# Splitting the remaining input projections of the second block's first mixer

## The chip, the core and the metric

The kernel runs on one NeuronCore of a Trainium2 chip. It is one launch for a whole network of two blocks of two layers each. The metric is the device time of one execution in microseconds (us); lower is better. The names of the engines are those of the profile: PE multiplies matrices, DVE is the vector engine, ACT the scalar engine, POOL does little here, and SP's queue issues the loads of the weights.

## The reference, cut to what matters

The first block (two layers) comes before the stretch that the change touches. The second block begins with `mixer_ab`, which projects the 256 tokens `x` (width 1024) by one wide matrix and feeds two attentions:

```python
def mixer_ab(x, w_in, gate_b, conv_w, head_g, w_out, rel_bias):
    p = jnp.einsum('bsd,de->bse', x, w_in)
    aq = p[..., AB_AQ:AB_AK].reshape(Bn, S, A_HEADS, A_HEAD_DIM)
    ak = p[..., AB_AK:AB_AV].reshape(Bn, S, A_HEADS, A_HEAD_DIM)
    av = p[..., AB_AV:AB_BQ].reshape(Bn, S, A_HEADS, A_HEAD_DIM)
    qk = jax.nn.silu(causal_conv(p[..., AB_BQ:AB_BV], conv_w))
    bq = qk[..., :B_WIDTH].reshape(Bn, S, B_HEADS, B_HEAD_DIM)
    bk = qk[..., B_WIDTH:].reshape(Bn, S, B_HEADS, B_HEAD_DIM)
    bv = p[..., AB_BV:AB_BO].reshape(Bn, S, B_HEADS, B_HEAD_DIM)
    bo = p[..., AB_BO:AB_BI]
    bi = p[..., AB_BI:AB_BF] + gate_b[:B_HEADS]
    bf = p[..., AB_BF:AB_PROJ] + gate_b[B_HEADS:]
    ya = dilated_attention(aq, ak, av, rel_bias).reshape(Bn, S, A_WIDTH)
    yb = jax.nn.sigmoid(bo.astype(jnp.float32)) * head_norm(mlstm(bq, bk, bv, bi, bf), head_g)
    y = jnp.concatenate([ya.astype(x.dtype), yb.astype(x.dtype)], axis=-1)
    return jnp.einsum('bse,ed->bsd', y, w_out)
```

The widths of aq, ak, av, bv and bo are 512 each, that of bq and bk together 1024. The first attention has 8 heads, the second 4. Everything is float32. After the mixer come a layer norm, a mixture of experts, and a second layer with another mixer.

## The kernel before

**The weight stream.** All weights lie in one stream of chunks of 128 x 1024 float32 (512 KB). SP loads them in order into a ring of 4 slots (line 2176). A slot is reloaded when the chunk in it was used. There are two ways to use a chunk.

- *Plain:* PE waits for the load and multiplies float32 by float32, straight from the ring. Each such matmul leaves two records in the profile (`XT,ring` or `ring,XT`). The slot is free (`weights_used`) when PE begins the next chunk.
- *Split:* ACT copies the chunk to `W_HI`, rounded to the type fp32r (line 1152); DVE writes the rest, chunk minus `W_HI`, to `W_LO` (line 1521), and the slot is free at that moment (`split_lo`). There are 4 pairs of `W_HI` and `W_LO`. The activations are split in the same way, here into `X_HI` and `X_LO`, once for all that use them (`split_x`). `mm` then issues three fp32r matmuls for each product: high by high, high by low, low by high.

`project` (line 555) makes one tile of 128 features by 256 tokens from one chunk with 8 products of 128 x 128 by 256. `tokens` (line 566) makes two tiles of 128 tokens by 512 features from 4 chunks, with 16 products of 128 x 128 by 512. `chunk` chooses plain or split by whether the activations come as a pair.

**Who splits when.** Each engine runs its own program, a walk over one list of steps (`schedule`, line 2205); an engine passes over the names for which it has no step. ACT and DVE put their splits between their other work by a `Follower`. PE's program is made first, and it notes a *mark* at each result (the key of its PSUM bank) and at the end of each step of the list: how many split chunks PE had begun there. When ACT or DVE pass the same mark in their own order, they first make all splits that the mark allows, that is up to three beyond the last one begun:

```python
def limit(self, mark):
    begun, n = self.marks[mark]
    count = min(begun - 1 + SPLIT, len(self.chunks))
...
def __call__(self, mark):
    while not self.paused and self.next < min(self.splits.limit(mark), self.ceilings[0]):
        self.one()
...
for name, *args in SCHEDULE:
    if name in steps:
        steps[name](*args)
    follow(("step", name, *args))
```

ACT passes a key's mark just behind the evacuation of that bank (`fn_free`), DVE behind its own reads of a bank (`free`). Both pass the step marks, also of the steps that they don't have. Each engine works strictly in its order: a split waits on ACT for its load and a free pair, on DVE for its `W_HI`, and all behind it waits too.

**The stretch of the change.** The order of the steps is:

- `ab_in`: aq (4 chunks), ak (4), av (4). Before the change the first aq chunk is plain (it comes while x is being split), the other seven of aq and ak are split, and av is plain. PE's line 786, ACT's line 1325.
- The first attention. For each head h: `a_scores(h+1)` (PE scores, DVE adds the bias and takes the maximum, ACT exponentials), `bqk_in(h)` (one chunk, the second attention's queries and keys; PE and ACT's evacuation alone, DVE has no such step), `a_norm(h)` (DVE: reciprocal of the sums and two scalings, line 1817), `a_turn(h)` (PE transposes the probabilities, ACT evacuates), and `a_values` behind every odd head.
- `if_in` (plain matmuls by a small matrix that lies in `PAR`), `b_gates` (DVE and ACT), `bo_in` (4 chunks, evacuated by ACT with a sigmoid), `b_conv` (DVE: 32 operations without a mark among them, then ACT's SiLU, then a scaling by DVE), `gate_rows`, `bv_in` (4 chunks).
- The second attention: `b_scores(0)`, and for each head `b_norm_weights`, `b_scores(h+1)`, `b_turn`, `b_values`; then `b_norm` and `y_out` (8 chunks, the first one plain, the others split).

Of the kernel before, what the change touches and what calls it, by code (L numbers as in the profile page):

```python
# [346 lines left out]
def build_program(nc, stream, params, consts, x_in, out, scratch):  # L347
    n_chunks = stream.shape[0] // 128
    with ExitStack() as ctx:
# [154 lines left out]
        def _(pe):  # L504
# [6 lines left out]
            def mm(dst, w, x, start=True, stop=True, done=None):  # L511


                if isinstance(w, tuple):
                    mm(dst, w[0], x[0], start, False)
                    mm(dst, w[0], x[1], False, False)
                    mm(dst, w[1], x[0], False, stop, done)
                    return
                ins = nc.tensor.matmul(dst, w, x, start=start, stop=stop, skip_group_check=True)  # L519
                if done is not None:  # L520
                    ins.then_inc(done, 1)
                    filled(done)
                elif state["release"]:
                    ins.then_inc(state["release"].pop(0), 1)
# [7 lines left out]
            def columns(w, lo, n):  # L532
                return tuple(p[:, lo : lo + n] for p in w) if isinstance(w, tuple) else w[:, lo : lo + n]

            def chunk(split=False, routed=None):

                n = state["n"]
                splits.place(routed)
                state["n"] += 1
                state["release"] += [state["held"]] if state["held"] is not None else []  # L540
                state["held"] = split_used if split else w_used
                if split:
                    i = len(splits.chunks)
                    splits.chunks.append(n)
                    pe.wait_ge(split_lo, i + 1)
                    return W_HI[:, i % SPLIT, :], W_LO[:, i % SPLIT, :]
                pe.wait_ge(arrived[splits.slot[n]], 16 * splits.turn[n])
                return ring_slot(n)

            def take(*key, bank=None):  # L550
                dst = banks.take(pe, key, bank)
                keys[banks.filled(key).name] = key
                return dst, banks.filled(key)

            def project(key, x, n=T, chunks=1, ready=None):

                dst, done = take(*key)
                for c in range(chunks):
                    w = chunk(isinstance(x(0), tuple))
                    for k in range(KT):  # L560
                        last = c == chunks - 1 and k == KT - 1
                        if ready is not None:
                            ready(8 * c + k)
                        mm(dst[:, :n], columns(w, 128 * k, 128), x(8 * c + k), c + k == 0, last, done if last else None)

            def tokens(key, x, tiles):

                dsts = [take(*key, i) for i in range(len(tiles))]
                for c in range(4):
                    w = chunk(isinstance(x(0, 0, 128), tuple))  # L570
                    splits.marks[(*key, "chunks")] = (len(splits.chunks), state["n"])
                    for i, (lo, n) in enumerate(tiles):
                        for k in range(2):
                            last = c == 3 and k == 1
                            mm(dsts[i][0][:n, :], x(2 * c + k, lo, n), columns(w, 512 * k, 512),
                               c + k == 0, last, dsts[i][1] if last else None)
# [27 lines left out]
            def till(name, before):  # L604

                return lambda k: pe.wait_ge(sem(name), before + k + 1)
# [173 lines left out]
            ht = lambda k: HT[:, k, :]  # L780
            x_parts = lambda k: (X_HI[:, k, :], X_LO[:, k, :])
            x_tok = lambda k, lo, n: (X_HI[:, k, lo : lo + n], X_LO[:, k, lo : lo + n])
            ht_tok = lambda k, lo, n: HT[:, k, lo : lo + n]
            TOK2 = [(0, 128), (128, 128)]

            def ab_in():
                for i, name in enumerate(("aq", "ak")):
                    for j in range(4):
                        project((name, j), x_parts if i + j else ht, 256,
                                ready=(lambda k: banks.await_read(pe, ("ff2", DEPTH - 1, 1, k)), till("x_split", 0))[j] if i == 0 and j < 2 else None)  # L790
                tokens(("av",), ht_tok, TOK2)

            def bqk_in(j):
                project(("bqk", j), ht, 256)

            def bo_in(j):
                project(("bo", j), ht, 256)

            def bv_in():
                tokens(("bv",), ht_tok, TOK2)  # L800

            def if_in():
                at = PARAMS["wif"][0]
# [339 lines left out]
        def _(act):  # L1143
# [10 lines left out]
            follow = Follower(splits, split)  # L1154
# [4 lines left out]
            def fn_free(dst, src, f, key, **kw):  # L1159

                nc.scalar.activation(dst, src, f, **kw).then_inc(banks.freed(key), 1)  # L1161
                banks.await_read(act, key)
                follow(key)

            def wait_bank(*key):
                return banks.await_(act, key)

            def evacuate(key, dst, n=T, f=ACT.Copy, rows=128, **kw):
                fn_free(dst, wait_bank(*key)[:rows, :n], f, key, **kw)
# [155 lines left out]
            def ab_in():  # L1325
                for j in range(4):
                    evacuate(("aq", j), AQ[:, j, :], 256, scale=A_SCALE)
                for j in range(4):
                    evacuate(("ak", j), AK[:, j, :], 256)
                for i in range(2):  # L1330
                    evacuate(("av", i), AV[:, i, :], 512)

# [1 line left out]
                evacuate(("bqk", j), BIN[:, j, 3:259], 256)  # L1334

            def bv_in():
                for i in range(2):
                    evacuate(("bv", i), BV[:, i, :], 512)

# [937 lines left out]
```

## Time and profile before

| | us |
|---|---|
| median of 3 runs (lowest, highest) | 2470.76 (2469.97, 2479.4) |
| the profiled execution, its own time | 2478.8 |
| its span, first to last instruction | 2476.9 |
| PE busy | 2289.2 (92%) |
| DVE busy | 1513.8 (61%) |
| ACT busy | 1067.9 (43%) |
| mean granted TensorE clock | 0.952 |

The span is that of one profiled execution. PE's busy time counts overlapping matmuls as one stretch, and their ends are modelled. The granted clock is a share of full speed. A bracket behind an instruction tells how long its engine was idle before it and which engine's work ended that.

### The profile page before, as it was taken

The numbers are of one execution on the slowest core, as the hardware profiler recorded it, in microseconds if no ns is written. First come the engines' busy times: TensorE is split into PE (matmuls) and PEld (weight loads), VectorE is DVE, ScalarE is ACT, GpSimd is POOL, SyncE is SP. The second block draws the span as 40 slices with busy tenths as digits, with TensorE's granted clock in tenths as the row PEclk, the third lists the DMA queues.
The fourth block names the chain that finished last, engine by engine and source line by source line (L and its number), as shares of the span: only waits on it lengthen the run. The fifth ranks groups of instructions, "written<-read, shape, count | busy, mean of one in ns | idle before, by whom it ended". The sixth has DMA issues, their size and how long they took to land.

```text
span 2476.9 us, 36662 instructions
## 1 busy us (share of the span) xinstructions
PE 2289.2 (92%) x13900; PEld 1911.1 (77%) x13900; DVE 1513.8 (61%) x2349; ACT 1067.9 (43%) x1514; POOL 232.4 (9%) x225
## 2 busy tenths in 40 slices
PE   7999898999999989899999779999989796999997
PEld 6677467999767756799976569987768476998775
DVE  2846365655375546676524565589975266658996
ACT  1142442443113244244333244467764254447775
POOL 1814000100271300011000000000000000000000
PEclk9999899999999989999999779999999898999999
DMA  4332123554333112355432134589964413458994
GB/s 156 128 120 77 51 69 119 179 179 170 111 128 117 63 51 77 136 188 189 162 132 97 43 109 146 197 291 348 345 230 171 136 44 112 151 190 319 346 353 178
DMA packets 109807, 396.86 MB, mean 160 GB/s; under 512 B 12088, under 2 KB 14144, under 8 KB 109376
## 3 DMA queue, kind: packets, MB, share of 16 engines
q1 hardware_dynamic: 108576, 393.45, 44.8%
q8 instruction: 111, 1.82, 0.3%
q10 hardware_dynamic: 1056, 1.06, 0.1%
q14 instruction: 64, 0.52, 0.1%
HBM read 393.40 MB, written 1.06 MB: 159 GB/s over the span
## 4 chain that ended last, share of the span: by engine, by line
PE 66%; DVE 20%; ACT 6%; DMA 5%; issue 2%; SPq 0%; DVEq 0%; ACTq 0%
PE psum L519 65%; DVE W_LO L1521 8%; DMA ring<-in_weights 4%; DVE region L1526 2%; ACT W_HI L1152 2%; PE psum L527 1%; DVE RS L1558 1%; DVE region L1529 1%; ACT region L1157 1%; DVE region L1533 1%; DVE SQ L1526 1%; ACT L1161 1%; ACT SQ L1157 1%; DVE HS L1993 1%; ACT L1157 0%
## 5 line engine op out<-in xcount | busy, mean ns | idle before, releaser
L1521 DVE TENSOR_TENSOR W_LO<-ring,W_HI 128x1024 fp32r<-128x1024 f32 x434 | 531.8, 1225 | 240.4 <-ACT W_HI L1152 232.1
L1152 ACT ACTIVATE W_HI<-ring 128x1024 fp32r<-128x1024 f32 x434 | 460.6, 1061 | 369.7 <-PE psum L519 233.5
L519 PE MATMUL psum<-HN,ring 128*128 128x272 f32 (+1 forms) x1600 | 383.7, 401 | 16.0 <-DVE HN L1533 16.0
L519 PEld LDWEIGHTS psum<-HN,ring 128*128 128x128 f32 x1600 | 310.6, 196 | 84.5 <-issue 24.9
L519 PE MATMUL psum<-X_HI,W_HI 128*128 128x256 f32 x800 | 230.0, 287 | 29.4 <-DVE W_LO L1521 26.6
L519 PE MATMUL psum<-X_LO,W_HI 128*128 128x256 f32 x800 | 227.2, 284 | 0.0
L519 PE MATMUL psum<-X_HI,W_LO 128*128 128x256 f32 x800 | 227.1, 284 | 0.0
L1161 ACT ACTIVATE region<-psum 128x272 f32<-128x272 f32 (+9 forms) x227 | 89.5, 394 | 277.1 <-PE psum L519 257.8
L1521 DVE TENSOR_TENSOR W_LO<-SQ,W_HI 128x1024 fp32r<-128x1024 f32 x128 | 156.8, 1225 | 41.1 <-ACT W_HI L1152 37.5
L519 PEld LDWEIGHTS psum<-X_HI,W_HI 128*128 128x128 f32 x800 | 155.7, 195 | 32.9 <-issue 23.2
L519 PE MATMUL psum<-FN_HI,W_HI 128*128 128x272 f32 (+1 forms) x592 | 170.1, 287 | 0.0
L519 PE MATMUL psum<-FN_HI,W_LO 128*128 128x272 f32 (+1 forms) x592 | 169.4, 286 | 0.0
L519 PE MATMUL psum<-FN_LO,W_HI 128*128 128x272 f32 (+1 forms) x592 | 169.1, 286 | 0.0
L1152 ACT ACTIVATE W_HI<-SQ 128x1024 fp32r<-128x1024 f32 x128 | 136.0, 1062 | 69.3 <-PE psum L519 59.4
L519 PE MATMUL psum<-W_HI,XG_HI 128*128 128x512 f32 x384 | 155.4, 405 | 10.0 <-DVE W_LO L1521 9.8
L519 PEld LDWEIGHTS psum<-X_HI,W_LO 128*128 128x128 f32 x800 | 154.6, 193 | 0.0
L519 PEld LDWEIGHTS psum<-X_LO,W_HI 128*128 128x128 f32 x800 | 154.4, 193 | 0.1
L519 PE MATMUL psum<-region 128*32 128x4 f32 (+12 forms) x1360 | 147.7, 252 | 7.2 <-ACT region L1161 5.6
L519 PE MATMUL psum<-W_HI,XG_LO 128*128 128x512 f32 x384 | 151.7, 395 | 0.0
L519 PE MATMUL psum<-W_LO,XG_HI 128*128 128x512 f32 x384 | 151.2, 394 | 0.0
L519 PE MATMUL psum<-F_HI,W_HI 128*128 128x272 f32 (+1 forms) x512 | 146.4, 286 | 0.1
L519 PE MATMUL psum<-F_HI,W_LO 128*128 128x272 f32 (+1 forms) x512 | 146.1, 285 | 0.0
(281 smaller groups left out, 4272.4 us busy)
## 6 DMA issues: line engine op xcount, KB each, us to landing
ring<-in_weights SPq DMA_DIRECT2D x615, 512.0 KB, 4.2
SQ<-in_weights SPq DMA_DIRECT2D x128, 512.0 KB, 5.2
XT<-in_x SPq DMA_DIRECT2D x1, 1088.0 KB, 5.0
CST<-in_consts SPq DMA_DIRECT2D x1, 1082.5 KB, 7.4
SQ<-bias_by_distance ACTq DMA_DIRECT2D x1, 1024.0 KB, 5.2
out<-XT SPq DMA_DIRECT2D x8, 128.0 KB, 1.9
PAR<-in_params SPq DMA_DIRECT2D x1, 572.0 KB, 8.3
bias_by_distance<-MIX ACTq DMA_DIRECT2D x1, 12.0 KB
```

Of the source, the lines that this page charges most:

```text
L519: ins = nc.tensor.matmul(dst, w, x, start=start, stop=stop, skip_group_check=True)
L527: ins = nc.tensor.transpose(dst, src, ident(k))
L1152: lane(nc.scalar.activation(W_HI[:, s % SPLIT, :], ring_slot(n), ACT.Copy), split_hi)
L1157: lane(nc.scalar.activation(dst, src, f, **kw), sem_)
L1161: nc.scalar.activation(dst, src, f, **kw).then_inc(banks.freed(key), 1)
L1521: lane(nc.vector.tensor_tensor(W_LO[:, s % SPLIT, :], ring_slot(n), W_HI[:, s % SPLIT, :].bitcast(F32), ALU.subtract), split_lo)
L1526: lane(nc.vector.tensor_tensor(dst, a, b, op), done)
L1529: ins = nc.vector.tensor_scalar(dst, a, s1, s2, op0) if op1 is None else nc.vector.tensor_scalar(dst, a, s1, s2, op0, op1)
L1533: lane(nc.vector.scalar_tensor_tensor(dst, a, s, b, op0, op1), done)
L1558: lane(nc.vector.reciprocal(ap, ap))
L1993: free(nc.vector.scalar_tensor_tensor(HS[:, :], src[:, :], SLOTG[:, g : g + 1], SGB[:, :], ALU.mult, ALU.mult), "moe", l, "up", e)
```

## The change

Four calls on PE get the split activations in place of the plain ones, so that 20 chunks become split ones: av (4), bqk (8), bo (4), bv (4). ACT passes the mark of the last chunk of av and of bv before it evacuates these two groups. Nothing else changes; order of steps, buffers and stream stay.

```diff
-                tokens(("av",), ht_tok, TOK2)
+                tokens(("av",), x_tok, TOK2)
 
             def bqk_in(j):
-                project(("bqk", j), ht, 256)
+                project(("bqk", j), x_parts, 256)
 
             def bo_in(j):
-                project(("bo", j), ht, 256)
+                project(("bo", j), x_parts, 256)
 
             def bv_in():
-                tokens(("bv",), ht_tok, TOK2)
+                tokens(("bv",), x_tok, TOK2)
@@ ACT, ab_in
                 for j in range(4):
                     evacuate(("ak", j), AK[:, j, :], 256)
+                follow(("av", "chunks"))
                 for i in range(2):
                     evacuate(("av", i), AV[:, i, :], 512)
@@ ACT
             def bv_in():
+                follow(("bv", "chunks"))
                 for i in range(2):
                     evacuate(("bv", i), BV[:, i, :], 512)
```

## Rows read from the trace of the kernel before

**Rows 1.** busy time by stage: us, PE, PEld, DVE, ACT, POOL busy, clock, DMA

```profile
1259.50:1273.40 13.90, 13.90 (x35) 5.97 (x33) 0.00 (x0) 0.98 (x2) 0.00 (x0) 1.00 0.31 111
1275.00:1318.00 43.00, 42.35 (x205) 32.76 (x204) 12.87 (x60) 18.20 (x52) 0.00 (x0) 1.00 0.29 99
1325.20:1353.50 28.30, 28.30 (x101) 18.40 (x100) 19.22 (x42) 9.75 (x13) 0.00 (x0) 1.00 0.43 147
...
1361.00:1388.50 27.50, 21.71 (x48) 12.22 (x48) 11.73 (x49) 6.22 (x14) 0.00 (x0) 0.50 0.00 0
```

**Rows 2.** order of time in the heads: start us, us, engine, what, idle before

```profile
1278.64 0.55 PE L527 MATMUL psum<-CST,GATE 128*128 128x128 f32 x3 [0.65 <-DVE GATE L1529]
1278.80 0.97 ACT L1161 ACTIVATE region<-psum 128x256 f32<-128x256 f32 x2
...
1279.12 0.92 PE L519 MATMUL psum<-region 64*128 64x128 f32 x4
...
1283.95 2.51 PE L519 MATMUL psum<-region 128*64 128x256 f32 x12
...
1287.28 0.17 DVE L1820 RECIPROCAL SM<-SM 128x2 f32<-128x2 f32 x1
...
1287.48 0.68 DVE L1529 TENSOR_SCALAR GATE<-GATE,SM 128x128 f32<-128x128 f32 x2
...
1289.95 0.49 PE L527 MATMUL psum<-CST,GATE 128*128 128x128 f32 x3
1290.21 0.91 ACT L1161 ACTIVATE region<-psum 128x256 f32<-128x256 f32 x2 [1.74 <-PE psum L519]
```

**Rows 3.** order of time from b_conv on, DVE and then PE

```profile
1331.89 0.36 DVE L1529 TENSOR_SCALAR region<-region,PAR 128x256 f32<-128x256 f32 x1
...
1345.94 1.53 DVE L1533 SCALAR_TENSOR_TENSOR region<-region,PAR 128x256 f32<-128x256 f32 x3
...
1351.58 0.17 DVE L1785 COPY region<-psum 128x16 f32<-128x16 f32 x1
...
1361.08 0.90 PE L527 MATMUL psum<-CST,GATE 128*128 128x128 f32 x3 [2.38 <-DVE GATE L1529]
...
1364.69 1.22 PE L519 MATMUL psum<-SQ,CST 4*128 4x256 f32 x2
...
1368.72 0.85 PE L527 MATMUL psum<-CST,GATE 128*128 128x128 f32 x3
```

**Rows 4.** order of time on ACT in the same stretch

```profile
1339.42 0.38 ACT L1161 ACTIVATE region<-psum 128x256 f32<-128x256 f32 x1 [3.07 <-PE psum L519]
...
1353.13 0.21 ACT L1157 ACTIVATE region<-region 128x8 f32<-128x8 f32 x1
```

**Rows 5.** order of time beside split chunks of ab_in, ACT and then DVE

```profile
1242.88 0.38 ACT L1161 ACTIVATE region<-psum 128x256 f32<-128x256 f32 x1 [6.87 <-PE psum L519]
1243.30 1.06 ACT L1152 ACTIVATE W_HI<-ring 128x1024 fp32r<-128x1024 f32 x1
1245.71 0.38 ACT L1161 ACTIVATE region<-psum 128x256 f32<-128x256 f32 x1 [1.35 <-PE psum L519]
...
1244.46 1.23 DVE L1521 TENSOR_TENSOR W_LO<-ring,W_HI 128x1024 fp32r<-128x1024 f32 x1 [2.35 <-ACT W_HI L1152]
```

**Rows 6.** order of time on PE, first and last of c_v's 48 matmuls

```profile
1908.29 0.40 PE L519 MATMUL psum<-W_HI,X_HI 128*128 128x512 f32 x1
...
1919.26 0.39 PE L519 MATMUL psum<-W_HI,X_LO 128*128 128x512 f32 x1
```

**Rows 7.** busy time and clock around two gaps of PE

```profile
170.00:178.00 8.00, 5.08 (x15) 3.92 (x15) 5.51 (x3) 7.71 (x13) 7.12 (x5) 0.79 0.17 62
1475.00:1479.00 4.00, 0.85 (x8) 0.66 (x7) 3.35 (x11) 2.32 (x3) 0.00 (x0) 1.00 0.00 0
1487.00:1491.00 4.00, 4.00 (x22) 4.00 (x21) 1.78 (x2) 1.64 (x3) 0.00 (x0) 0.57 0.39 131
```

**Rows 8.** the page's DMA issues: size and us to landing

```profile
ring<-in_weights SPq DMA_DIRECT2D x615, 512.0 KB, 4.2
```

## The prediction, made before the changed kernel ran

> **What bounds the kernel now.** I read the stages' busy times first [rows 1]. From the value projection on (1259.5 us) the busy share of PE is everything: the eight heads of the first attention (1275 to 1318) have PE at 42.35 of 43.00 us, and gate plus values of the second attention (1325.2 to 1353.5) at 28.30 of 28.30. All of it runs at the full granted clock. DVE and ACT are at 30 to 42% in the heads. Then I read the order of time inside a head [rows 2]: PE goes from turning the probabilities to scores to the next bqk chunk without a break, and DVE's normalising (1287.48, over at 1288.2) is ready 1.8 us before PE wants it at 1289.95. Last I read DVE and ACT of the second attention's start [rows 3, 4]: there PE's bo and bv chunks run beside a DVE chain of almost the same length (b_gates, 15.6 us of b_conv, SiLU, scaling).
>
> **What the change saves on PE.** A plain project chunk costs PE 3.46 us: ACT's evacuation of the last bo (1339.42) is 0.38 long and comes after 3.07 idle, one chunk of PE [rows 4]. A split one costs 2.83 us: the evacuations at 1242.88 and 1245.71 [rows 5]. So 0.63 us less for each of 12 chunks. The plain av group fills 13.9 us [rows 1]; the split c_v group of the same shape goes from 1908.29 to about 1919.5 [rows 6], 48 matmuls at 0.234 = 11.2 us. So 2.7 us less for av and for bv. Were this all, the PE saving would be 12 x 0.63 + 2 x 2.7 = 12.9 us.
>
> **What it adds.** 20 chunks need a W_HI on ACT (1.06 us) and a W_LO on DVE (1.23 us) [rows 5], 21 and 25 us in sum. The idle shares would hold them; their place in the queues does not. Both followers take the split that is three chunks ahead as soon as their own program passes a mark that PE recorded. ACT passes the first mark that allows it, that of ("bqk", h), after evacuating bqk h. DVE has no step bqk_in; it passes the step mark of bqk_in(h), which allows the same split, straight after a_scores(h+1) and before a_norm(h). No earlier mark allows it (the a_scores(h+1) keys were recorded before bqk h was begun). So W_LO waits there for a W_HI that waits for the end of bqk h, behind it stands a_norm(h), and on PE a_turn(h) waits for a_norm(h), with scores of h+2 and bqk h+1 queued behind it. This wait is new, and it is inside the loop.
>
> Its price per head, from the moment PE could go on: 0.26 us to the start of the evacuation (PE goes on at 1289.95, ACT starts at 1290.21 [rows 2]), 0.42 to W_HI's start, 1.16 to W_LO's start, 1.23 of W_LO with 0.03 after it [rows 5], 0.20 from the reciprocal to the scaling and 0.68 of scaling [rows 2], 0.05 to PE: 4.05 us in which PE has nothing. Less the 0.63 saved, each of heads 1 to 7 gets 3.42 us longer: 23.9 us. For head 0 ACT is busy until 1278.80 (a table load and four exponentials); its evacuation of 0.42 starts there, then 0.42 + 1.16 + 1.26 + 0.88 + 0.05 = 3.77, puts the turn at 1282.57 against 1278.64 [rows 2]: 3.9 us. **Heads: +27.8 us.** Bounds of this term: 0 less 5 us saved, if DVE had W_LO behind it in time, and nothing above, since each link has its row. In av the extra follow(("av", "chunks")) lets ACT split before it evacuates, as c_in does: no wait, **-2.7 us**.
>
> **The clock.** The kernel before has such gaps elsewhere: in the 8 us from 170 on PE is busy for 5.08, after a gap of 2.9, and the granted clock is 0.79. Between the two levels (1.2 and 2.4 GHz, 0.50 and 1.00) that makes 0.21 x 2 x 8 = 3.4 us at half. From 1475 PE has 0.85 us of work in 4; the same 3.4 us at half (0.43 x 2 x 4) come there too, but only from 1487 on, beside a full PE [rows 7]. Work that falls into 3.4 us at half speed loses up to 1.7 us. The eight gaps of 4.05 us are of this size. A part of the low stretch lies in the gap itself, and it may also last longer than 3.4 us with only 4 to 6 us of work between gaps. I take 1.7 us for each: **+13.6 us**; bounds 0 and, at 0.50 all through, once more the PE work of the heads (turn 0.42, scores 0.85, bqk 2.83 = 4.1 us, and in every odd head the values, 2.51 - 0.92 = 1.59 more [rows 2]), 39 us.
> The Trainium skill, page "TensorE: Matmul & The Clock Gate", section "HAM oscillation — how this bites in real kernels", says that where every round waits longer than it works, TensorE starts every round at the lower clock. Here the wait (4.05) is about as long as the work (4.1 to 5.7). By the page every round starts slow, and the term is at least the one taken, at most rival (b); the trace's single gaps agree, and no row shows a repeated one.
>
> **Gate and values of the second attention.** All from the end of if_in, 1325.3. Before: DVE starts b_conv at 1331.89, needs 15.6 us (8 groups, 1331.89 to 1347.5), SiLU with table load, scaling and copy to 1351.75, that is 26.45 [rows 3]. After: DVE must do four W_LO, the ones three ahead of bo 0 to 3, between b_gates and b_conv, and the last of them follows the end of bo 3. PE: bo 0 to 3 at 2.83 = 11.3; then 0.26 + 0.42 + 1.16 + 1.26 = 3.1: b_conv starts at 14.4, 7.85 late. The fourth bv chunk has its W_LO only at DVE's step bv_in, behind b_conv; and its W_HI on ACT behind SiLU and the table load for the floors (free 1.6 us after the copy [rows 4]). PE stands still after the third bv chunk, from about 20 to 38. Counting from the copy (34.3): W_HI 1.65 to 2.7, W_LO to 4.0, bv's last chunk 4.0 to 9 or 9.6 (2.8 us at full, 5.6 at half clock). Meanwhile both engines run three more splits: of the last, the ring slot is free at 4.0, its load lands 4.2 later [rows 8], W_HI to 9.4, W_LO to 10.65, and only then may DVE mask the scores of head 0. b_scores(0) and (1) take PE 8.1 us at half clock (4.03 for one, 1364.69 to 1368.72 [rows 3]), about half at full. b_turn(0) thus comes at 14 (full) to 17.6 (half) after the copy, against 9.3 before (1361.08). I take 15.9. **7.85 + 6.6 = +14.4 us**; bounds +12.5 and +16.2, or -2 if the splits were free.
> From b_turn(0) on nothing changes: that part sits at 0.50 already [rows 1], its splits are done, and y_out's first chunk stays plain, so the ring is held where it was.
>
> **Sum.** 27.8 - 2.7 + 13.6 + 14.4 = +53 us. Against the profiled execution (span 2476.9, 2478.8 in all) that is 2532; it ran 8 us above the median of its three runs, and the median is what I add to: 2470.76 + 53 = 2524.
>
> **Rivals.**
> (a) The clock stays full in the heads and in bv's last chunk: 27.8 - 2.7 + 12.5 = +37.6, 2508. For it: after the gap at 1475 the clock stayed full for eight microseconds more [rows 7]. Against: the fall came all the same.
> (b) The clock stays at half all through the heads: 27.8 - 2.7 + 39 + 16.2 = +80, 2551. For it: 1361 to 1388.5 is at 0.50 all the way with PE 79% busy [rows 1]. Against: a round of the heads has bqk's dense matmuls in it, and with such work behind the gap the half clock lasted 3.4 us in both places [rows 7]. The Trainium skill's rule above (page "TensorE: Matmul & The Clock Gate") leads here if a round that starts slow also stays slow.
> (c) The other side: the new W_LO does not stand in the way, since DVE and ACT have 58 to 70% of their time free. Its mechanism is that each split is done one head earlier than I read it, in the time that DVE idles (it has 12.87 us of work in 43 [rows 1]). Then the heads give 8 x 0.63 = 5 us, av 2.7, and bo and bv no more than 2, since the chain over DVE ends at 1351.54 and PE's values at 1353.5, 1.96 us later: 2461. It decides if a_norm(h) comes before the end of bqk h; the order of marks speaks against it.
> (d) Only one of the two places stalls: b_conv alone 14.4 - 2.7 - 5 = +7, 2477; the heads alone 27.8 + 13.6 - 2.7 - 2 = +37, 2507.
>
> **Chances.** Forecast 0.62 (its own range 2512 to 2540), (a) 0.14, (b) 0.10, (c) 0.06, (d) 0.08. Range for 8 in 10: 2503 to 2547. Half a per cent is 12 us, about what a measurement tells from no change: slower 0.91, same 0.04, faster 0.05.
>
> **What would show it.** In the heads: gaps of about 4 us before PE's turn, released by DVE's scaling; DVE idle before W_LO, released by ACT; PE share near 50 to 60%; clock 0.6 to 0.9 there. After if_in: four W_LO between the gate rows and b_conv, DVE's first convolution some 14.4 us after if_in, a PE gap of about 18 us inside bv that ends with W_LO. Wrong if the normalising starts before bqk ends, or if b_conv starts 6.6 us after if_in.

## The result, and the profile after

The changed kernel takes 2535.09 us (median of 6 runs, 2526.53 to 2541.37), the one before 2473.6 (6 runs, 2469.97 to 2483.88): 1.0239 times as long, interval 1.0216 to 1.0262, or 61.5 us more. The profiled execution took 2532.66 with a span of 2530.8, against 2478.8 and 2476.9 before; its mean granted clock is 0.934 against 0.952. The page after, span, busy times and the two kinds of split instruction:

```profile
span 2530.8 us, 36998 instructions
...
PE 2298.4 (91%) x14028; PEld 1932.5 (76%) x14028; DVE 1537.9 (61%) x2369; ACT 1089.2 (43%) x1534; POOL 232.0 (9%) x225
...
L1523 DVE TENSOR_TENSOR W_LO<-ring,W_HI 128x1024 fp32r<-128x1024 f32 x454 | 556.2, 1225 | 285.6 <-ACT W_HI L1152 277.2
L1152 ACT ACTIVATE W_HI<-ring 128x1024 fp32r<-128x1024 f32 x454 | 481.9, 1061 | 372.4 <-PE psum L519 232.9
```

Each split costs what the prediction's rows say (1.23 and 1.06 us), and neither DVE nor ACT is short of time. The stages show where the time went. Windows of the kernel after, columns as in [rows 1]: av; the heads from the first turn to the last; the last turn with if_in; from there to b_turn(0); the first heads of the second attention:

```profile
1258.80:1270.00 11.20, 11.20 (x52) 8.95 (x52) 6.44 (x6) 6.28 (x7) 0.00 (x0) 1.00 0.70 231
1279.00:1361.90 82.90, 55.89 (x237) 46.31 (x237) 19.68 (x58) 21.24 (x48) 0.00 (x0) 0.64 0.13 45
1361.90:1373.50 11.60, 11.56 (x44) 4.98 (x44) 0.47 (x1) 0.87 (x2) 0.00 (x0) 0.74 0.13 47
1373.50:1422.30 48.80, 30.75 (x165) 24.78 (x166) 32.65 (x68) 20.78 (x26) 0.00 (x0) 0.79 0.16 54
...
1422.30:1448.80 26.50, 21.06 (x49) 12.14 (x47) 10.71 (x44) 5.64 (x13) 0.00 (x0) 0.50 0.00 0
```

The av group takes 11.2 us where it took 13.9 [rows 1]. From the first turn (of the probabilities of head 0) to the last the heads take 82.9 us where they took 37.6 (1278.64 in [rows 2] to the first row below); PE is busy for 55.9 of the 82.9, at a clock of 0.64 where it was 1.00 [rows 1]. The last turn and if_in take 2.5 us more (the turn to if_in's end was 9.0), b_turn(0) comes 48.8 us after if_in where it came 35.8 after (1325.3 to 1361.08 [rows 3]). The last row answers to the last of [rows 1], and is much as it was (PE busy for 79% in both, clock 0.50). The turn of head 7, before and after:

```profile
1316.23 0.49 PE L527 MATMUL psum<-CST,GATE 128*128 128x128 f32 x3
```

```profile
1361.94 0.90 PE L527 MATMUL psum<-CST,GATE 128*128 128x128 f32 x3 [3.86 <-DVE GATE L1531]
```

One head of after in order of time (start us, us, engine, what, in brackets the idle time before it and what ended that), to be read against [rows 2]:

```profile
1299.92 0.28 PE L519 MATMUL psum<-X_HI,W_LO 128*128 128x256 f32 x1
1300.30 0.39 ACT L1161 ACTIVATE region<-psum 128x256 f32<-128x256 f32 x1 [3.19 <-PE psum L519]
1300.71 1.06 ACT L1152 ACTIVATE W_HI<-ring 128x1024 fp32r<-128x1024 f32 x1
1301.87 1.23 DVE L1523 TENSOR_TENSOR W_LO<-ring,W_HI 128x1024 fp32r<-128x1024 f32 x1 [5.99 <-ACT W_HI L1152]
...
1303.13 0.17 DVE L1822 RECIPROCAL SM<-SM 128x2 f32<-128x2 f32 x1
1303.33 0.68 DVE L1531 TENSOR_SCALAR GATE<-GATE,SM 128x128 f32<-128x128 f32 x2
...
1304.06 0.90 PE L527 MATMUL psum<-CST,GATE 128*128 128x128 f32 x3 [3.86 <-DVE GATE L1531]
```

bqk ends, its evacuation follows, W_HI follows that, W_LO follows W_HI, and the reciprocal, for which everything had been ready long before (DVE idle for 5.99 us), follows W_LO. PE waits 3.86 us. The waits of the whole stretch (engine, tile, what it waited for: us in sum, times, longest), after:

```profile
DVE W_LO L1523 <- ACT W_HI L1152: 41.5, 7, 7.6
...
PE psum L527 <- DVE GATE L1531: 28.5, 7, 5.3
```

and before, from the first turn to the last:

```profile
PE psum L527 <- DVE GATE L1529: 0.7, 1, 0.7
```

The 28.5 hold head 0's gap (5.3, which ends where the stretch begins) and six of 3.86. Head 7's gap, of 3.86 too, ends with the stretch and is not counted in them: inside the 82.9 us lie seven, 27.0 us. What the gaps do to the clock shows in windows of 2 us over one head, columns as before:

```profile
1304.00:1306.00 2.00, 1.94 (x7) 1.43 (x7) 0.19 (x2) 0.49 (x1) 0.00 (x0) 0.50 0.74 262
1306.00:1308.00 2.00, 2.00 (x9) 1.53 (x8) 0.79 (x5) 0.50 (x2) 0.00 (x0) 0.50 0.02 4
1308.00:1310.00 2.00, 2.00 (x11) 2.00 (x11) 0.00 (x0) 0.60 (x2) 0.00 (x0) 0.52 0.00 0
1310.00:1312.00 2.00, 1.07 (x10) 0.88 (x8) 0.00 (x0) 0.80 (x2) 0.00 (x0) 1.00 0.00 0
1312.00:1314.00 2.00, 0.00 (x0) 0.00 (x0) 1.23 (x1) 0.64 (x1) 0.00 (x0) 0.83 0.00 0
1314.00:1316.00 2.00, 1.06 (x4) 0.74 (x5) 0.80 (x3) 0.08 (x1) 0.00 (x0) 0.50 0.49 141
```

PE starts the round at 0.50 and does nearly all of it so; the full clock comes back at 1310, when 1.07 us of work are left, is spent on an idle engine, and is gone by the next turn. So it goes in all seven rounds (a round is the time from one turn to the next): the full clock comes back when 0.4 to 1.3 us of work are left, and falls again while PE waits.

The second place, DVE and PE between if_in's end (1373.5) and b_turn(0), against [rows 3]:

```profile
1380.08 2.48 DVE L1523 TENSOR_TENSOR W_LO<-ring,W_HI 128x1024 fp32r<-128x1024 f32 x2
1383.54 1.22 DVE L1523 TENSOR_TENSOR W_LO<-ring,W_HI 128x1024 fp32r<-128x1024 f32 x1 [0.98 <-ACT W_HI L1152]
1386.26 1.23 DVE L1523 TENSOR_TENSOR W_LO<-ring,W_HI 128x1024 fp32r<-128x1024 f32 x1 [1.49 <-ACT W_HI L1152]
1387.52 0.35 DVE L1531 TENSOR_SCALAR region<-region,PAR 128x256 f32<-128x256 f32 x1
...
1407.21 0.17 DVE L1787 COPY region<-psum 128x16 f32<-128x16 f32 x1
1410.15 3.74 DVE L1523 TENSOR_TENSOR W_LO<-ring,W_HI 128x1024 fp32r<-128x1024 f32 x3 [2.77 <-ACT W_HI L1152]
1415.92 1.22 DVE L1523 TENSOR_TENSOR W_LO<-ring,W_HI 128x1024 fp32r<-128x1024 f32 x1 [2.02 <-ACT W_HI L1152]
1417.18 0.29 DVE L1528 TENSOR_TENSOR GATE<-psum,CST 128x128 f32<-128x128 f32 x1
```

```profile
1411.43 0.80 PE L519 MATMUL psum<-W_HI,X_HI 128*128 128x512 f32 x1 [18.05 <-DVE W_LO L1523]
...
1422.27 0.85 PE L527 MATMUL psum<-CST,GATE 128*128 128x128 f32 x3
```

Four W_LO stand ahead of the first convolution, which starts 14.0 us after if_in (before 6.6); after the copy four more stand ahead of the masking, PE has waited 18.05 us for the first of them, and b_turn(0) comes 14.9 us after the end of the copy (before 9.3).

So by places, in the profiled executions: av -2.7, head 0's turn +3.9 (av's start to it: 19.06 before, 20.24 after), the other heads +45.3, last turn and if_in +2.5, to b_turn(0) +13.0. Sum +62.0, and the medians differ by 61.5. That the two agree to half a microsecond is partly luck: from b_turn(0) to the end the profiled executions of the twelve kernels of this document take anything from 1106.0 to 1118.8 us (before 1115.8, after 1108.5).

### The profile page after: what moved, and what is told of

Its sections match the earlier page's. It is cut to its first block, busy times and chain, and to the rows that moved or that the text cites. A ratio compares the mean times of both kernels' runs of the same rounds, so it can differ in the third digit from the quotient of the medians.

```text
span 2530.8 us, 36998 instructions
## 1 busy us (share of the span) xinstructions
PE 2298.4 (91%) x14028; PEld 1932.5 (76%) x14028; DVE 1537.9 (61%) x2369; ACT 1089.2 (43%) x1534; POOL 232.0 (9%) x225
## 3 DMA queue, kind: packets, MB, share of 16 engines
q10 hardware_dynamic: 1056, 1.06, 0.1%
HBM read 393.40 MB, written 1.06 MB: 156 GB/s over the span
## 4 chain that ended last, share of the span: by engine, by line
PE 68%; DVE 18%; ACT 6%; DMA 5%; issue 2%; SPq 0%; DVEq 0%; ACTq 0%
PE psum L519 67%; DVE W_LO L1523 6%; DMA ring<-in_weights 4%; ACT W_HI L1152 2%; DVE region L1528 2%; PE psum L527 2%; DVE RS L1560 1%; DVE region L1531 1%; ACT region L1157 1%; DVE region L1535 1%; ACT L1161 1%; DVE SQ L1528 1%; ACT SQ L1157 1%; DVE GATE L1531 0%; DMA SQ<-in_weights 0%
## 5 line engine op out<-in xcount | busy, mean ns | idle before, releaser
L1523 DVE TENSOR_TENSOR W_LO<-ring,W_HI 128x1024 fp32r<-128x1024 f32 x454 | 556.2, 1225 | 285.6 <-ACT W_HI L1152 277.2
L1152 ACT ACTIVATE W_HI<-ring 128x1024 fp32r<-128x1024 f32 x454 | 481.9, 1061 | 372.4 <-PE psum L519 232.9
L519 PE MATMUL psum<-X_HI,W_HI 128*128 128x256 f32 x896 | 262.8, 293 | 27.2 <-DVE W_LO L1523 25.2
L519 PE MATMUL psum<-X_LO,W_HI 128*128 128x256 f32 x896 | 258.3, 288 | 0.0
L519 PE MATMUL psum<-X_HI,W_LO 128*128 128x256 f32 x896 | 257.7, 288 | 0.0
L519 PEld LDWEIGHTS psum<-X_HI,W_HI 128*128 128x128 f32 x896 | 179.0, 200 | 34.9 <-issue 27.7
L519 PEld LDWEIGHTS psum<-X_LO,W_HI 128*128 128x128 f32 x896 | 178.8, 200 | 0.1
L519 PEld LDWEIGHTS psum<-X_HI,W_LO 128*128 128x128 f32 x896 | 178.8, 200 | 0.0
L519 PE MATMUL psum<-region 128*32 128x4 f32 (+12 forms) x1360 | 153.4, 259 | 6.7 <-ACT region L1161 4.9
```

Source lines behind the costliest of these rows:

```text
L1152: lane(nc.scalar.activation(W_HI[:, s % SPLIT, :], ring_slot(n), ACT.Copy), split_hi)
L1523: lane(nc.vector.tensor_tensor(W_LO[:, s % SPLIT, :], ring_slot(n), W_HI[:, s % SPLIT, :].bitcast(F32), ALU.subtract), split_lo)
```

## The experiments

Two theories stand against each other: that W_LO's place in DVE's queue makes the wait, and a clock that falls with it the rest (mine); and that the splits' cost is in the engines' work itself, or in the split matmuls. Edits are against the changed kernel. For each I give the same three stretches, next to what they are before and after: from av's first matmul to head 0's turn (before 19.06, after 20.24), from there to head 7's turn (37.59, 82.92), and from the end of if_in to b_turn(0) (35.8, 48.8). The kernel before ran beside each of them; its medians lie between 2473.3 and 2478.5.

### 1. The W_LO in the loop placed behind the normalising

DVE takes no split at the mark of bqk_in, and so takes it at the next step, a_norm:

```
-                follow(("step", name, *args))
+                if name != "bqk_in":
+                    follow(("step", name, *args))
```

> The changed kernel, but DVE passes the mark of bqk_in(h) only together with that of a_norm(h), so W_LO stands behind the normalising and not ahead of it. Nothing else moves. Theory 1 (the place of W_LO costs the time in the heads): the eight PE gaps of 3.9 us shrink to 1 us or less (W_LO now delays the mask of the next head, some 3.1 us after bqk ends), the clock stays near 1.00 in the heads, turn(0) to turn(7) falls from 82.9 us to 34 to 42 (37.6 before the change), and the total is some 45 to 50 us under the changed kernel, +10 to +15 over the kernel before (ratio about 1.005). Rival (the amount of added work on ACT and DVE costs the time, wherever it stands): turn(0) to turn(7) stays over 70 us, ratio about 1.02. The stretch from the end of if_in to b_turn(0) stays at 48.8 us by both.

2489.79 us (2485.43 to 2495.25), 1.0068 times before (1.0043 to 1.0093). The stretches: 16.3, 42.65, 48.8. Some 45 of the 61.5 us hung on where one instruction of 1.23 us stands. But the heads did not fall under 37.59, and they and the total lie just above what was expected: PE still waits 0.6 to 0.8 us before every other turn and 0.99 or 1.00 before the values that follow, and in one head the clock fell, which made its round 9.94 us long where other rounds with values took 6.83. Windows: the heads, then four of 2 us in that head:

```profile
1281.50:1324.20 42.70, 36.80 (x238) 30.13 (x238) 19.63 (x58) 22.12 (x52) 0.00 (x0) 0.92 0.22 75
1312.00:1314.00 2.00, 1.49 (x5) 0.77 (x5) 1.23 (x1) 0.46 (x1) 0.00 (x0) 0.61 0.00 0
1314.00:1316.00 2.00, 2.00 (x7) 1.35 (x7) 0.52 (x3) 0.38 (x1) 0.00 (x0) 0.50 0.71 262
1316.00:1318.00 2.00, 2.00 (x11) 2.00 (x11) 1.19 (x6) 1.10 (x4) 0.00 (x0) 0.50 0.00 0
1318.00:1320.00 2.00, 2.00 (x14) 2.00 (x13) 0.00 (x0) 0.00 (x0) 0.00 (x0) 0.68 0.00 0
```

The short gaps come from the same link, one step on. DVE, in another head of it:

```profile
1295.12 1.23 DVE L1523 TENSOR_TENSOR W_LO<-ring,W_HI 128x1024 fp32r<-128x1024 f32 x1 [2.93 <-ACT W_HI L1152]
...
1296.38 0.29 DVE L1814 CUSTOM_DVE_ANT_0 GATE<-psum,BIAS_A 128x128 f32<-128x128 f32 x1
```

W_LO waits for the W_HI of the bqk just done, and DVE's work on the next scores, for which the next turn waits, starts behind it at 1296.38. The gaps of 1 us are ACT's: in the order that the change left it, W_HI (1299.01 to 1300.07) stands ahead of the evacuation of the turned probabilities (1300.10), for which PE's values wait.

### 2. The gap filled with matmuls that nobody needs

Before each turn PE does nine matmuls of 256 columns (and one small one that ends the group) into a bank of their own. Their result is used by nothing; they only stand in the gap.

```
+                dst, done = take("keep", h)
+                for k in range(9):
+                    mm(dst[:, :256], ones(128, 128), ht(k % KT), k == 0, k == 8, done if k == 8 else None)
...
```

> The changed kernel, and PE in addition multiplies without use between bqk h and turn h: nine float32 matmuls of 128x128 by 256 (about 3.9 us at full clock) into a bank of its own, which nobody reads. Theory 1a (of the 45 us that the heads lost, 22.6 are the gaps themselves and the rest is the granted clock, which falls in each gap): PE has no gap, the clock stays at 1.00, turn(0) to turn(7) falls from 82.9 to about 62 us, if_in to its old length, and the total is 20 to 25 us under the changed kernel (ratio about 1.014), though PE does 35 us more work. Rival (the rounds are long for another wait, the clock only follows): the heads stay at 80 us or more, and the total is the same or higher.

2508.89 us (2507.38 to 2511.57), 1.0146 times before (1.0117 to 1.0175): 26 us less than the changed kernel, with more work. The stretches: 20.25, 61.43, 47.6. The window of the heads:

```profile
1278.90:1340.30 61.40, 61.40 (x377) 51.15 (x377) 19.72 (x58) 21.28 (x48) 0.00 (x0) 1.00 0.18 61
```

No idle time and a clock of 1.00. The DVE chain is untouched, it is only covered. The heads of experiment 4 have the same split work, no gaps and full clock, and take 32.89 us. Against them the filler takes (61.43 - 32.89) / 7 = 4.08 us a head, 0.22 more than the gap. So the clock's price in the seven rounds of after is 82.92 - 61.43 = 21.5, and 7 x 0.22 = 1.5 more: 23.0 us.

### 3. Only av split

```
-                project(("bqk", j), x_parts, 256)
+                project(("bqk", j), ht, 256)
-                project(("bo", j), x_parts, 256)
+                project(("bo", j), ht, 256)
-                tokens(("bv",), x_tok, TOK2)
+                tokens(("bv",), ht_tok, TOK2)
-                follow(("bv", "chunks"))
```

> Only av is split (and ACT passes its mark ahead of the evacuation); bqk, bo and bv are plain. Theory: the av group 11.2 us and not 13.9, no new gap anywhere, heads 37.6 us from turn(0) to turn(7); the total 2.7 us lower, which one look does not show. Rival (the ACT mark ahead of the evacuation delays the first exponentials): turn(0) comes no earlier than before relative to the start of av (19.1 us).

2471.52 us, a single run. The stretches: 16.32, 37.58, 35.8. Too small for one run to tell from no change, but the trace has it: the group takes 11.2 us, and nothing behind it is late.

```profile
1257.80:1269.00 11.20, 11.20 (x52) 8.95 (x50) 2.83 (x3) 3.10 (x4) 0.00 (x0) 1.00 0.47 151
```

### 4. av and bqk split, each split one head later

bo and bv plain; ACT takes no W_HI at bqk_in, a_norm and the turns of odd heads, nor DVE a W_LO in the steps of a head, until behind a_norm, and then the one of the head before:

```
+                if name == "a_norm" and args[0]:
+                    follow.paused = False
+                    follow(("step", "a_norm", args[0] - 1))
...
```

> A try for a version that beats both: av and bqk split, bo and bv plain as before the change; in the heads DVE does the W_LO of the chunk three ahead of bqk h-1 behind a_norm(h), one head later than its mark allows, and ACT does W_HI behind the evacuation of the turned probabilities (behind that of the values in odd heads). Theory 1: no gaps, av 2.7 us shorter, 8 x 0.63 = 5 us shorter heads, gate and values unchanged: 7 to 8 us under the kernel before (ratio 0.997). Rival (ACT and DVE have no room even in the right order): gaps of 1 us or more in each head, and no gain or a loss.

2470.3 us (2459.75 to 2474.12, 12 runs), 0.9981 times before (0.9961 to 1.0). The stretches: 16.32, 32.89, 35.8. The window of the heads, and one head of it:

```profile
1284.90:1317.80 32.90, 32.78 (x238) 27.73 (x239) 17.19 (x56) 19.28 (x48) 0.00 (x0) 1.00 0.24 81
```

```profile
1291.83 1.06 ACT L1152 ACTIVATE W_HI<-ring 128x1024 fp32r<-128x1024 f32 x1
...
1293.19 0.68 DVE L1530 TENSOR_SCALAR GATE<-GATE,SM 128x128 f32<-128x128 f32 x2
...
1293.90 1.23 DVE L1522 TENSOR_TENSOR W_LO<-ring,W_HI 128x1024 fp32r<-128x1024 f32 x1
```

Here W_LO finds its W_HI done a microsecond before, stands behind the scaling, and is free. The heads are 4.7 us shorter than before: 7 times 0.63 would be 4.4. So the split matmuls themselves are worth what the prediction said, if nothing waits. W_HI on ACT was moved here too, so this experiment does not tell its share from W_LO's; in experiment 1 both kinds of gap still stand side by side.

### 5. av and bqk split, DVE's mark as changed

The edit of 3 without its first two lines, so that bqk is split.

> av and bqk split as in the changed kernel, with DVE's mark where it is there; bo and bv plain as before. Theory 1 (each wait of a_norm(h) comes from the one split three chunks ahead): only the chunks of bqk 3 to 7 are left to split in the heads, so the gaps of 3.9 us stand before turn 0 to 4 and not before turn 5 to 7; turn(0) to turn(4) takes 49 us as in the changed kernel, turn(4) to turn(7) about 13 us against 33.7 there, gate and values are as before the change (b_turn(0) 35.8 us after if_in), total +26 us over the kernel before (ratio 1.010). Rival (all eight heads lose because bqk's own split matmuls or the splits of x make them slow): turn(5) to turn(7) keep gaps, ratio 1.018 or more.

2507.67 us (2503.81 to 2508.88), 1.0124 times before (1.0093 to 1.0156). The stretches: 20.25, 64.36, 35.8. With bo plain, nothing is left to split three chunks ahead of bqk 5 to 7, and there the gaps are missing: turns 1 to 4 wait 3.86 us each, turns 5 to 7 not at all. The two parts of the heads, up to turn 4 and from it:

```profile
1280.20:1329.10 48.90, 33.46 (x140) 27.19 (x140) 11.80 (x36) 12.87 (x30) 0.00 (x0) 0.64 0.13 44
1329.10:1344.50 15.40, 15.38 (x97) 13.24 (x98) 4.22 (x19) 4.82 (x14) 0.00 (x0) 0.82 0.10 34
```

Rounds with a gap run at the same clock of 0.64 whether four or seven follow each other; when the gaps stop, the clock is back at 1.00 within the next round. That round ran at half for 5.5 of its 6.7 us, so that turn 4 to turn 7 took 15.4 us where 13 were expected. The heads' loss is so much per gap, wait and clock both.

### 6. av, bo and bv split, bqk plain, DVE's mark as in 1

> av, bo and bv split, bqk plain, and DVE passes the mark of bqk_in(h) only with that of a_norm(h). This isolates the second place, gate and values. Theory 2 (four W_LO ahead of b_conv, and bv's last W_LO behind it): heads as before the change within 3 us, b_conv starts 14 us after the end of if_in instead of 6.6, an 18 us gap of PE inside bv, b_turn(0) 48.8 us after if_in instead of 35.8, total +13 - 2.7 = +10 us over the kernel before (ratio 1.004). Rival (this stretch was late only because the heads before it were): b_turn(0) at most 37 us after if_in, and the total 2 to 3 us under the kernel before.

2489.35 us (2484.95 to 2498.45), 1.0059 times before (1.0031 to 1.0086). The stretches: 16.33, 39.04, 48.8. The second place costs its 13.0 us with no gap of 3.86 in the heads: the two places are independent. The heads are 1.5 us longer than before and the last turn with if_in 0.7, since the first W_HI for bo stand ahead of evacuations in heads 5 to 7 and PE waits for these, 1.02 us once and 0.59 once. The total is 16 us over the kernel before, where 10 were expected; the traces give 12.5 of them (see the sums).

### 7. All split, the W_LO of bo and bv spread inside b_conv

The heads as in 4, and in b_conv:

```
+                    if j % 2 == 0:
+                        follow(("step", "bo_in", j // 2))
...
```

> All 20 chunks split, the heads in the order of e4_av_bqk_lag, and DVE's W_LO of bo's and bv's marks spread between the groups of b_conv (one behind groups 0, 2, 4 and 6, and bv's last behind group 6), with ACT's W_HI of bv's last chunk ahead of its wait for b_conv. So nothing waits for the end of a chunk of PE and bv is not held behind b_conv; what is left is the amount, five W_LO of 1.26 us in the chain over DVE. Theory 2 (in gate and values the amount counts, since the DVE chain ends last there even before the change): b_conv starts 6.6 us after if_in and takes 22 us, b_turn(0) comes 42 us after if_in (35.8 before, 48.8 in the changed kernel), the total is within 3 us of the kernel before (ratio 1.000), 3 to 7 us above e4_av_bqk_lag. Rival (here too only the place counts): b_turn(0) at 34 to 36 us after if_in and the total 8 to 10 us under the kernel before.

2477.33 us (2469.46 to 2493.75, 12 runs), 1.0009 times before (0.9989 to 1.003). The stretches: 16.5, 32.8, 42.7. b_conv starts 6.6 us after if_in again, and lasts longer by the W_LO in it. DVE, first rows:

```profile
1327.40 0.35 DVE L1532 TENSOR_SCALAR region<-region,PAR 128x256 f32<-128x256 f32 x1
...
1329.35 1.22 DVE L1524 TENSOR_TENSOR W_LO<-ring,W_HI 128x1024 fp32r<-128x1024 f32 x1
```

Five W_LO lie in it now, and it ends 6.3 us later than before; the other 0.6 come behind the copy, where DVE makes three W_LO and not two. So here, where the chain over DVE ends last, a W_LO costs its own time even when it waits for nothing. That no other placing could bring this stretch back to 35.8 is argued and not shown: this is the only one that was run with bo and bv split and b_conv started in time (9 has the same), and none used another engine for W_LO.

### 8. As 4, and the two splits for y_out behind head 0's weights

Before the change already, two W_LO for y_out stand ahead of the masking of the second attention's head 0. Here ACT and DVE pass them over at bv_in and b_scores(0), DVE at b_norm_weights(0) too.

```
+ ... or name == "bv_in" or (name, *args) == ("b_scores", 0)
```

> e4_av_bqk_lag, and in addition ACT and DVE keep the two splits of y_out out of the chain at the start of the second attention (they come behind head 0's exponentials and weights, not ahead of its mask). Theory (what stands ahead in a queue costs, also in the kernel before): DVE masks head 0 some 3 us earlier, b_turn(0) comes 32 to 33 us after if_in and not 35.8, the total is 10 to 11 us under the kernel before (ratio 0.996). Rival (the mask waits for the evacuation of bv or for PE's scores anyway): b_turn(0) at 35 to 36 us, ratio 0.997 to 0.998 as e4_av_bqk_lag.

2467.97 us (2456.51 to 2475.82, 10 runs), 0.9966 times before (0.9948 to 0.9984). The stretches: 16.3, 32.89, 33.0. b_turn(0) is 2.8 us earlier, b_turn(1) only 0.2 (43.2 against 43.4 after if_in), and the total is 7.4 us under the kernel before, where 10 to 11 were expected. ACT, DVE and PE rows say why:

```profile
1349.48 0.51 ACT L1157 ACTIVATE GATE<-GATE,region 128x256 f32<-128x256 f32 x1 [2.70 <-DVE GATE L1527]
```

```profile
1346.44 2.48 DVE L1522 TENSOR_TENSOR W_LO<-ring,W_HI 128x1024 fp32r<-128x1024 f32 x2
```

```profile
1350.56 1.65 PE L519 MATMUL psum<-region 128*128 128x256 f32 x4 [3.65 <-ACT region L1161]
```

The two W_LO now stand between the two maskings of head 1, ACT waits 2.70 us for the second, and with the turned probabilities of head 0 queued behind it PE gets them 3.65 us late: the wait went one head on.

### 9. As 7, with the edit of 8

> e7_inter with the same two pauses: all 20 chunks split, three y_out splits behind head 0's weights. Theory 2 (in gate and values the five W_LO inside b_conv are what is left): b_turn(0) 39 us after if_in (42.7 in e7_inter, less some 3.5), so still 6 us later than in e8_late; total 3 to 4 us under the kernel before (ratio 0.9985), some 6 us over e8_late. Rival (with the queues in order the saving of bo and bv on PE shows): e9 at or below e8_late.

2479.84 us (2470.08 to 2485.65, 10 runs), 1.0009 times before (0.9993 to 1.0024). The stretches: 16.33, 32.89, 38.5; then 11.4 to b_turn(1), since three W_LO for y_out (3.74 us) now stand between the two maskings of head 1. The same as 7 in time, for the reason of 8. Expected were 3 to 4 us under the kernel before and some 6 over 8; the medians say 4.5 over the one and 11.9 over the other, the traces 0.9 under and some 7 over.

### 10. As 8, with DVE's two W_LO behind head 1's weights too

```
+                if (name, *args) == ("b_norm_weights", 1):
+                    follow.paused = False
+                    follow(("step", "bv_in"))
```

> e8_late with the two y_out W_LO one more head back: behind head 1's weights and ahead of head 2's mask (in e8_late they stood between the two masks of head 1, ACT's exponential waited for them, and behind it the evacuation of head 0's turned probabilities: b_turn(1) came 10.2 us after b_turn(0) instead of 7.6). Theory: b_turn(0) 33 us and b_turn(1) 41 us after if_in (43.2 in e8_late, 43.4 before the change), total 2 to 3 us under e8_late, 10 us under the kernel before (ratio 0.996). Rival (the wait moves on again, to head 2's mask): b_turn(2) 50 us or more after if_in, as before the change (50.5), and a total equal to e8_late's.

2462.69 us (2456.59 to 2465.45, 6 runs), 0.9935 times before (0.991 to 0.996): 12.1 us under the kernel before, 72 under the changed one. The stretches: 16.31, 32.8, 33.0; b_turn(1) is 39.1 us after if_in (before 43.4), b_turn(2) 46.6 (50.5). PE waits 1.48 us where it waited 3.65. A row of DVE, then one of PE:

```profile
1358.72 2.48 DVE L1522 TENSOR_TENSOR W_LO<-ring,W_HI 128x1024 fp32r<-128x1024 f32 x2
```

```profile
1357.37 0.92 PE L519 MATMUL psum<-region 128*128 128x256 f32 x4 [1.48 <-ACT region L1161]
```

### The sums

The stretches' differences from before (with b_turn(1) instead of b_turn(0) in 8 to 10) against those of the medians:

| kernel | from the traces, us | medians, us |
|---|---|---|
| after | -2.7 +3.9 +45.3 +2.5 +13.0 = +62.0 | +61.5 |
| 1 | -2.7 +5.1 +13.1 = +15.5 | +16.5 |
| 2 | +1.2 +23.8 +11.8 = +36.8 | +35.6 |
| 4 | -2.7 -4.7 = -7.4 | -3.0 |
| 5 | +1.2 +26.8 = +28.0 | +29.2 |
| 6 | -2.7 +1.5 +0.7 +13.0 = +12.5 | +16.0 |
| 7 | -2.5 -4.8 +6.9 = -0.4 | -1.1 |
| 8 | -2.7 -4.7 -0.2 = -7.6 | -7.4 |
| 9 | -2.7 -4.7 +6.5 = -0.9 | +4.5 |
| 10 | -2.7 -4.8 -4.3 = -11.8 | -12.1 |

Where the two differ by 3.5 to 5.4 us (4, 6, 9), the interval of the ratio holds the sum from the traces (-9.6 to 0, 7.7 to 21.3, -1.7 to 5.9 us). The ratios given with the experiments are estimates of their own and not the quotients of the medians: 7 is 1.1 us under by its median and 1.0009 by its ratio, and either means no difference.

## Why the prediction was right

Forecast 2524, measured 2535.09 us: slower, at the two places and for the reasons it gave, inside its range, 11 us above its number. Of these 11, 2.8 come from the base (it added to 2470.76, the median of three runs; six runs give 2473.6, and 2535.09 - 2473.6 is 61.5), the other 8.5 from its terms. By its steps:

- **What PE saves.** Right. av 2.7 us (3), a bqk chunk 0.63 by the forecast and 4.7 us over seven heads measured (4).
- **The new wait in the loop.** Right in place, cause and size: 4.05 us expected (its terms add up to 4.03), 3.86 measured, seven times. Head 0's was to be 3.9 and is 3.9. Net of the saving the eight heads cost 7 x 3.86 - 7 x 0.63 + 3.9 = 26.5 us where 27.8 stood. Experiment 1 shows the cause (the same split one step later, and the waits are gone but for 0.6 to 0.8 us), experiment 5 shows it from the other side (no split due, no wait).
- **The clock.** The right mechanism, and the one term that was mis-sized: 1.7 us for each of eight gaps, 13.6, was taken. Over the seven rounds the after kernel's 82.92 us less 7 x 3.86 of gaps leave 55.9 of work, which at full clock takes 32.9 (4): 23.0 us for the clock, 3.3 a round; the last turn and if_in add 2.5. Together 25.5, so 11.9 too little. I had the low stretch as 3.4 us after one gap [rows 7] and let half a round lie at full clock. In the repeated case the stretch is longer: at a mean of 0.64 over 82.9 us, 0.36 x 2 x 82.9 = 60 us ran at half, 8.5 a round. Laid over PE's busy times, 50.2 of the 55.9 us of work fell into it, 7.2 of 8.0 a round. The 23.0 rest on experiment 4's heads, and so do the 23.0 of experiment 2, where 32.89 is in the sum again; by rows of its own experiment 2 gives 23.2: the filler takes 4.11 us from its first matmul to the turn (1283.06 to 1287.17), and 61.43 - 7 x 4.11 = 32.7 is left for the work at full clock.
  Rival (b), half all through, put 39 us on this. As a number that was further off than 13.6, in mechanism it was nearer, since PE spent nine tenths of its busy time at half. Two things made its price too high. It took half clock for twice the time, and this work took 1.85 times: the 50.2 us hold 32.9 - 5.7 = 27.2 us of work at full clock (a turn takes 0.90 us for 0.49, and split matmuls of 256 columns start 0.213 apart for 0.114). And it counted 39 us of work in eight rounds, where the seven rounds hold 32.9 and the eighth adds only the 2.5. That the forecast came closer to the total than (b) is thus in part luck: 2524 and 2551 lie on either side of 2535.
  The Trainium skill (page "TensorE: Matmul & The Clock Gate", section "HAM oscillation — how this bites in real kernels") was weighed here. By its rule, a loop that waits longer than it works pays the slow start in every round, not once. The trace of after agrees, though here wait (3.86) and work at full clock (4.1 to 6.0 in experiment 4, 3.1 in the last round) are about equal: all eight turns take 0.90 us, where one took 0.49 or 0.55 before [rows 2]. I gave it the smaller price; it deserved the larger.
- **Gate and values of the second attention.** Right: b_conv was to start 14.4 us after if_in and starts 14.0 after; the PE gap in bv was to be about 18 us and is 18.05; b_turn(0) was to be 15.9 us behind the copy and is 14.9. In sum +14.4 was said, +13.0 came. The last chunk did run at half clock for most of its matmuls, at 0.43 us apart and from 1415.8 on at 0.23. Experiment 6 shows this term by itself.
- **"From b_turn(0) on nothing changes."** The pace of the next heads is as it was (b_turn(0) to b_turn(3): 19.77 us before, 19.50 after). In the two profiled executions the lag is 61.2 us at b_turn(0) and 53.9 at the end; some 5.5 of it go between 1453 and 1616. Over the twelve profiles b_turn(0) to the end takes 1106.0 to 1118.8 us, and both kernels lie within that; the medians give 61.5. So I take it for the scatter of single executions. No run was made to settle that.
- **Rivals.** (a), a clock that stays full, is refuted by the 0.64 of the heads; it gave 2508. (c), the splits fall into idle time, needs the normalising to come before W_LO. It does not. Experiment 4 brings that about by another way (each split one head later, where (c) had it one earlier), and it gives what (c) said for the heads (-4.7 of -5 us). (d), one place alone, is 5 and 6: +29 us with five of the eight gaps, and +16, where 37 (all eight) and 7 were given. My 7 held 5 us of savings in the heads, which a kernel with plain bqk cannot have.

The sum: 53 forecast, -1.3 for the gaps, +11.9 for the clock, -1.4 for the second place: 62.2, where 61.5 was measured.

## What to carry to other kernels

Work fetched ahead is not free because its engine is idle: in a queue kept in order it costs as long as it must wait for its own input, and everything behind it pays. Look for the first instruction behind it that somebody waits for, and put it there; here one W_LO moved by one step was worth 45 us, and both halves of the splits moved further, W_LO by one head, another 10 in the heads (42.65 in 1, 32.8 in 7, all 20 chunks split in both). Where the queue's own chain ends last, as in b_conv, even a split that waits for nothing costs its time. When a loop on TensorE gets a gap of about the size of its work (here 3.86 us and 4.7), price the clock for nearly the whole round and not for a moment after the gap.

## What the runs showed that I had not expected

- The clock falls in with the gaps: in the heads of after it comes back when 0.4 to 1.3 us of a round's work are left, and goes while PE is idle. So it is in all seven rounds, and it costs 3.3 us in each.
- Work that nobody needs made the kernel 26 us faster (2508.89 against 2535.09), since it held the clock at 1.00 for 61.4 us where it had been 0.64.
- A gap need not be 4 us to cost clock: in experiment 1 gaps of 0.6 to 0.8 us before every second turn, with another of 0.99 before the values of the odd heads, went without harm for five rounds, and in the sixth the clock was at 0.50 for 6.8 us. That these gaps made it fall is inferred: in the kernels without them (4, 7 to 10) it stayed at 1.00 through the heads, but no run changes the gaps alone.
- A wait taken from one head can appear almost whole in the next (8): b_turn(0) 2.8 us earlier, b_turn(1) 0.2.
